# Embedding matmuls moved into the expert groups of a hybrid decoder step, eight expert pieces loaded beside the ring instead of six

## What is computed

```python
h = h + mix
h = h + hier_moe(rmsnorm(h, norm_ffn[i]), ...)
h = h + (p[i] @ ple_w_in[i]) * jax.nn.sigmoid(rmsnorm(h, ple_g[i]) @ ple_w_gate[i])
# in hier_moe: a group of 8 experts by argmax, the top 2 in it, then
a = jnp.einsum('btd,edf->btef', h, w_gate)
u = jnp.einsum('btd,edf->btef', h, w_up)
return jnp.einsum('btef,efd->btd', jax.nn.silu(a) * u * gates[..., None], w_down)
```

## Time and profile before

| | |
|---|---|
| median of 3 runs | 950.71 us (944.7 to 959.28) |
| profiled execution | 951.04 us, span 949.3 us |
| mean granted TensorE clock | 0.921 of 2.4 GHz |
| PE busy | 785.6 us, 83% |
| DVE, ACT, POOL busy | 321.6, 206.6, 56.2 us |
| moved by DMA | 269.32 MB, mean 284 GB/s |

### The profile page before, as it was taken

The page is one execution under the profiler, slowest core; times in us unless marked ns, Lnnn a source line. Parts: engine busy times, 40 slices in busy tenths (PEclk is TensorE's granted clock), DMA queues, the critical chain, the costliest instruction groups (busy, mean ns, idle before and its releaser), DMA issues.

```text
span 949.3 us, 16693 instructions
## 1 busy us (share of the span) xinstructions
PE 785.6 (83%) x6434; PEld 569.2 (60%) x6434; DVE 321.6 (34%) x948; ACT 206.6 (22%) x490; POOL 56.2 (6%) x95
## 2 busy tenths in 40 slices
PE   5899889999777796989997685798998787878894
PEld 4767568765453464667774362587755455545683
DVE  1512333523131331255265272226232231313435
ACT  2100131621111111132135251015211110111222
POOL 3300000000000000000033232000000000000000
PEclk9989998999988988999999796799998898899997
DMA  9941826499999999974319164468699999999501
GB/s 370 368 111 51 266 76 257 164 394 408 415 417 416 415 418 415 419 317 137 129 58 348 33 222 154 164 235 314 271 401 421 414 418 417 416 415 416 220 1 46
DMA packets 59613, 269.32 MB, mean 284 GB/s; under 512 B 7312, under 2 KB 12704, under 8 KB 38416
## 3 DMA queue, kind: packets, MB, share of 16 engines
q1 hardware_dynamic: 53088, 259.31, 69.1%
q10 hardware_dynamic: 3856, 5.40, 1.9%
q0 software_dynamic: 2592, 3.54, 1.2%
HBM read 261.05 MB, written 2.52 MB: 278 GB/s over the span
## 4 chain that ended last, share of the span: by engine, by line
PE 49%; DMA 26%; issue 13%; POOLq 4%; DVE 4%; ACT 2%; ACTq 1%; POOL 1%; SPq 1%; DVEq 0%
DMA ring<-in_moe_w_up 22%; PE bank L623 15%; PE bank L483 13%; PE bank L602 6%; POOLq L1857 3%; PE bank L649 3%; PE bank L507 3%; PE bank L664 2%; DMA arena<-in_stateT 2%; PE bank L892 2%; DMA arena<-arena 1%; PE bank L544 1%; PE bank L558 1%; POOLq L1859 1%; POOLq L1856 1%
## 5 line engine op out<-in xcount | busy, mean ns | idle before, releaser
L623 PE MATMUL bank<-ring,arena 128*32 128x256 f32 x2048 | 148.2, 436 | 62.6 <-DMA ring<-in_moe_w_up 60.2
L623 PEld LDWEIGHTS bank<-ring,arena 128*32 128x32 f32 x2048 | 86.5, 125 | 129.9 <-issue 107.6
L483 PE MATMUL bank<-xn_sq,ring 128*128 128x264 f32 x480 | 109.8, 391 | 10.3 <-DVE xn_sq L996 10.3
L483 PE MATMUL bank<-arena,ring 128*128 128x264 f32 (+1 forms) x456 | 108.7, 399 | 6.5 <-ACT arena L1597 4.0
L483 PEld LDWEIGHTS bank<-xn_sq,ring 128*128 128x128 f32 x480 | 92.2, 193 | 27.1 <-issue 11.1
L1229 DVE TENSOR_TENSOR arena<-arena,bank 128x128 f32<-128x128 f32 x34 | 9.8, 288 | 287.7 <-ACT arena L1638 287.7
L483 PEld LDWEIGHTS bank<-arena,ring 128*128 128x128 f32 x456 | 89.8, 198 | 23.4 <-issue 7.0
L602 PEld LDWEIGHTS bank<-arena 128*128 128x128 f32 x864 | 97.9, 192 | 9.4 <-issue 9.4
L602 PE MATMUL bank<-arena 128*128 128x128 f32 (+1 forms) x864 | 101.1, 277 | 2.0 <-DVE arena L1199 2.0
L649 PE MATMUL bank<-ring,arena 128*32 128x512 f32 x512 | 65.4, 598 | 16.6 <-ACT arena L1645 16.4
L664 PE MATMUL bank<-arena 128*128 128x264 f32 (+1 forms) x288 | 70.7, 399 | 4.7 <-ACT arena L1654 4.7
(11 more groups left out here) (243 smaller groups left out, 799.1 us busy)
## 6 DMA issues: line engine op xcount, KB each, us to landing
ring<-in_moe_w_gate SPq DMA_DIRECT2D x60, 1024.0 KB, 13.9
ring<-in_moe_w_up SPq DMA_DIRECT2D x60, 1024.0 KB, 10.8
ring<-in_moe_w_down SPq DMA_DIRECT2D x60, 1024.0 KB, 12.9
ring<-in_stream SPq DMA_DIRECT2D x35, 1024.0 KB, 14.4
ring<-in_cache_ckv SPq DMA_DIRECT2D x32, 256.0 KB, 7.4
arena<-in_moe_w_down SPq DMA_DIRECT2D x4, 1024.0 KB, 13.4
arena<-in_cache_ckv SPq DMA_DIRECT2D x16, 256.0 KB, 4.3
xn_sq<-in_cache_ckv SPq DMA_DIRECT2D x16, 256.0 KB, 6.1
```

Source lines behind the costliest of these rows:

```text
L483: t = mm(ps[:, 0:cols], lhs(k), rhs(k), start=(k == 0), stop=(k == n - 1))
L623: t = mm(bank[2 + r][p0:p0 + U, 0:F].rearrange("p (c f) -> p c f", c=2), x, w[i][:, :, k * F + c * P:k * F + (c + 1) * P], start=(k == 0), ...
```

## The change

The embedding weights leave the ring. They have an array of their own (`a["pin"]`) and are loaded in the expert stage, behind ring piece i = 26 (`PIN_AT`), into arena buffer 5, once expert 5 is used. The embedding matmuls leave the router part and stand in groups 3 to 6, two chunks each, between `down(a)` and `gate_up(b)`. They write banks 6 and 7, and `pinT` now lies over arena buffers 3 and 4. ACT copies the two chunks behind `pair_out(a)`, and `combine(j)` and the final embedding wait for the copies.

The room of `pinT` and 952 columns more in the arena give six arena buffers instead of four. `ASIDE` has eight pieces: expert 3, the down piece of expert 2, gate and up of expert 5, gate and up of expert 4. The ring list has 88 pieces for 90: i = 6 and 7 are gate and up of expert 2, i = 8 and 9 the down pieces of experts 4 and 5, and the blocks of six begin at i = 10. Ahead of the stage nine ring pieces and eight aside are loaded, 17 for 15. The six in the arena are issued after the last taps of layer 0 (after the first output chunk of attention in layer 1) instead of behind the last output chunk. Four small router tables move into the used tap table `wq`.

```diff
--- before.py
+++ after.py
@@ -44,7 +44,7 @@
 NSLOT = 9
-ARENA = 21888
+ARENA = 22840
@@ -82,12 +82,12 @@
-MOE_PIECES = both(0) + [(e, c) for e in (2, NSTAT) for c in range(3)]
+MOE_PIECES = both(0) + [(2, 0), (2, 1), (4, 2), (5, 2)]
 for _e in range(NSTAT + 1, E, 2):
 RING_AT = {piece: i for i, piece in enumerate(MOE_PIECES)}
-ASIDE = [(3, 0), (3, 1), (3, 2), (4, 2), (4, 0), (4, 1)]
+ASIDE = [(3, 0), (3, 1), (3, 2), (2, 2), (5, 0), (5, 1), (4, 0), (4, 1)]
...
@@ -225,9 +225,11 @@
         gatesT, q = place(q, 2, T)
-        pinT, q = place(q, KD, T)
-        aside, q = place(q, 4, SLOT)
-        assert q <= ARENA
+        aside_at = q
+        aside, q = place(q, 6, SLOT)
+        assert q <= ARENA, q
+        pinT, _ = place(aside_at + 3 * SLOT, KD, T)
+        win = aside[:, 5, :].rearrange("p (k f) -> p k f", k=2)
         aside_x = xn_sq[:].rearrange("p a b c -> p (a b c)")[:, 0:2 * SLOT].rearrange("p (c f) -> p c f", c=2)
...
@@ -415,20 +420,20 @@
-            if e in (3, 4):
-                return aside[:, 0:2, :] if e == 3 else aside_x
+            if e in (3, 4, 5):
+                return {3: aside[:, 0:2, :], 4: aside_x, 5: aside[:, 4:6, :]}[e]
             i = (G_MOE[l] + RING_AT[e, 0]) % NSLOT
-            if e in (3, 4):
-                return aside[:, e - 1, :]
+            if e in (2, 3):
+                return aside[:, 5 - e, :]
             return slot(G_MOE[l] + RING_AT[e, 2])
-            if e in (3, 4):
+            if (e, c) in ASIDE:
                 eng.wait_ge(s_aside[e, c], 16 * (l + 1))
@@ -558,16 +563,6 @@
-                win = slot(G_PIN[l]).rearrange("p (k f) -> p k f", k=2)
-
-                def pin(ms):
-                    for m in ms:
-                        chunk(("pin", l, m), 2, lambda k: win[:, k, m * P:(m + 1) * P], lambda k: pT[:, l, k, :])
-
-                pe.wait_ge(s_p, 16)
-                landed(pe, G_PIN[l])
-                pin(range(5))
-
                 ps = open_bank(pe, ("cnt", l))
@@ -582,8 +577,6 @@
                 t.then_inc(is_full(("rank", l)), 1)
-                pin(range(5, KD))
-
                 for b in range(8):
@@ -650,9 +643,23 @@
+                def pin(j):
+
+                    pe.wait_ge(s_win, 16 * (l + 1))
+                    pe.wait_ge(s_p, 16)
+                    pe.wait_ge(s_add, KD * (gb + j - 1) + 6)
+                    for x in range(2):
+                        m = 2 * (j - 3) + x
+                        for k in range(2):
+                            t = mm(bank[6 + x][:, 0:T], win[:, k, m * P:(m + 1) * P], pT[:, l, k, :], start=(k == 0),
+                                   stop=(k == 1))
+                        t.then_inc(s_pin, 1)
+
                 def combine(j):
                     n = cols_of(j)
+                    if 3 <= j < 7:
+                        pe.wait_ge(s_pinned, KD * l + 2 * (j - 2))
                     pe.wait_ge(s_out, 2 * (pb + min(2 * j + 2, NPR)))
@@ -680,6 +687,8 @@
                     down(a)
+                    if 3 <= j < 7:
+                        pin(j)
                     gate_up(b)
@@ -1356,6 +1365,7 @@
                 name = "n3" if l == 0 else "n6"
+                dve.wait_ge(s_pinned, KD * (l + 1))
                 for m in range(KD + 1):
@@ -1613,12 +1623,8 @@
                          .then_inc(is_free(key), 1)
-                for m in range(5):
-                    pin_in(l, m)
                 act.wait_ge(s_pre, l + 1)
                 s.activation(ex[:], ex[:], ACT.Exp).then_inc(s_ex, 1)
-                for m in range(5, KD):
-                    pin_in(l, m)
                 pb, gb = NPR * l, NGR * l
@@ -1675,6 +1681,14 @@
                     pair_out(a)
+                    if 3 <= j < 7:
+                        if j == 3:
+                            act.wait_ge(s_dn, pb + 2)
+                            act.wait_ge(s_gu, pb + 3)
+                        for x in range(2):
+                            m = 2 * (j - 3) + x
+                            act.wait_ge(s_pin, KD * l + m + 1)
+                            s.copy(pinT[:, m, :], bank[6 + x][:, 0:T]).then_inc(s_pinned, 1)
                     silu(b)
@@ -1944,22 +1951,23 @@
                 e, c = ASIDE[i]
-                d = aside_x[:, c, :] if i >= 4 else aside[:, i, :]
+                d = aside_x[:, c, :] if i >= 6 else aside[:, i, :]
                 if c == 2:
-                for i in range(NSLOT - 1):
+                for i in range(5):
                     load_expert(l, i, MOE_PIECES[i][0])
-                arrive(sp, (("pw2" if l == 0 else "wo"), KD - 1))
-                for i in range(4):
+                arrive(sp, ("taps", KD - 1) if l == 0 else ("wo", 0))
+                for i in range(6):
                     load_aside(l, i)
+                for i in range(5, NSLOT):
+                    load_expert(l, i, MOE_PIECES[i][0])
                 arrive(sp, ("row", l, 2, 1))
-                for i in range(4, 6):
+                for i in range(6, 8):
                     load_aside(l, i)
-                load_expert(l, NSLOT - 1, MOE_PIECES[NSLOT - 1][0])
                 sp.wait_ge(s_perm, l + 1)
@@ -1967,6 +1975,10 @@
                     load_expert(l, i, number[e])
+                    if i == PIN_AT:
+                        sp.wait_ge(s_dn, NPR * l + 2)
+                        sp.wait_ge(s_gu, NPR * l + 3)
+                        sp.dma_start(aside[:, 5, :], a["pin"][l]).then_inc(s_win, 16)
...
@@ -1985,7 +1997,7 @@
                     load_cache(SB * B + i, numbers[i])
-            for g in range(G_PIN1 - 1, G_MOE1):
+            for g in range(G_MOE1 - 1, G_MOE1):
                 fill(g)
```

34 lines of the change are left out of this document (16 added, 18 removed).

## The result

The changed kernel takes 960.72 us, the median of 4 runs (957.9 to 963.78). The kernel before took 950.17 us beside it (4 runs, 944.7 to 959.28). The ratio is 1.0139, with a 95% interval of 1.0088 to 1.0189: slower, by less than 2%. The ratio compares only executions in the faster of the two states that the chip shows, so it is not the quotient of the two medians. The profiled execution took 961.9 us, its span 959.8 us, at a mean granted clock of 0.924. The forecast of 954 had the sign, but a third of the size: +3.4 us were forecast, against +10.5 us by these medians and +10.9 us by the two profiled executions.

The account below looks back on a forecast made before the run. Expert stages were taken as bound by DMA loads, restarting after the router part. Per layer -1.3 (start) and +3.0 (DMA) give +1.7, +3.4 for two layers: 954 us from 950.7; own range 950 to 959, 8 in 10 within 945 to 961.

Parts of the forecast that it names:

- the cold gather: First gather behind the router part: starts at half clock after TensorE idles, costing 1.7 us a layer (0 to 2.0).
- the DMA side of the stream: Expert stage, from the restart of the loads to pair 15: 3.0 us longer per layer (3.0 to 4.0).
- Counts 3.0 us earlier: Router part: without the embedding matmuls ahead of them, the count matmuls start 3.0 us sooner in each layer.
- Router gain: Router part: expert loads restart 1.3 us earlier per layer, 3.0 us from earlier counts less 1.7 for the slow gather.
- The hole: Expert loads after the restart: the ninth waits for pair 2's down matmuls and lands 7.95 us after the eighth, 5.4 lost.
- Early loads: Six arena pieces loaded earlier, at 112 us and about 614 us, where DMA has room: zero cost.
- Embedding matmuls in the stage: Groups 3 to 6: four matmuls of 1.85 us per group fit in the DMA wait ahead of gate_up(b), zero cost.
- Embedding weights at 2.5 us: Expert stage, behind piece 26: loading the embedding weights adds one transfer, 2.5 us per layer.
- Outside the stages: All time outside the router part and the expert stream: no term in the sum, forecast difference 0.
- clock holds: Rival for the router part: full clock through the short matmuls, -3.0 + 3.0 per layer, total 951, chance 0.17.
- no hole: Rival for the expert loads: the stream never runs dry, -3.8 us per layer, total 943.4, chance 0.13.
- Groups held up: Rival for groups 3 to 6: embedding matmuls and their chain of waits delay the groups, total 970, chance 0.05.

Follow-up runs that it names:

- the fourth experiment: The changed kernel with its six early arena loads issued behind the last output chunk again, as in the kernel before: 960.34 us, ratio 1.0106.

## Why the prediction was off

The mechanisms were right: the counts came sooner, the gather ran cold, the stream had a hole. What failed is the sum. Two of its terms were too small: the cold gather (1.7 us against 2.7) and the DMA side of the stream (3.0 us a layer against 3.6). A third, the time outside the two stages, was put at nothing without a reason. The first two make 2.8 us and are shown by traces and experiments. The third is 1.2 us in the traces, within their scatter; another 3.8 us (11.2 less 7.4) are seen in the timed executions alone, have no place in any trace, and their cause stays open.

- **Counts 3.0 us earlier: right.** From DVE's step on the router's logits to the counts it took 5.1 us instead of 8.0 (8.3 in layer 1). In the two experiments with a warm gather and nothing in its way (unread matmuls; chunks spread) the router part is 2.6 to 3.1 us shorter than in the first profile of before.
- **The cold gather: mechanism right, size wrong.** I took 1.7 us from a gate-up behind a 4.75 us wait, and 2.0 as the upper end. It was 2.7 (8.33 and 8.34 against 5.61). The row I priced it by was one in which the clock came back sooner. Here the low clock held until 182, 5.9 us into the gather, so about half of its 5.6 us of work was done at half speed, and the upper end "half of four slow microseconds" was too small. The end of the ranks was slow too (2.00 us against 1.64). Router gain: 0.5 us a layer in place of 1.3. The Trainium skill's page "TensorE: Matmul & The Clock Gate", section "HAM oscillation — how this bites in real kernels", says that a wait which lets the array fall back makes the next burst start cold. The trace agrees in that the gather starts at a PEclk of 0.50 in both layers, but here the clock had fallen ahead of the wait, during the ranks, and the size of 2.7 us had to come from a run.
- **The hole: right in place and mechanism, low by 0.6 us a layer.** Ninth load 26.70 us behind the first (26.85 forecast), 7.6 us between the landings (7.95), pair 6 17.5 us behind pair 5 (17.6), pair 5 at 53.4 and 53.2 us (242.8 - 189.65 = 53.15 forecast). At pair 15 the DMA side was 3.1 us longer in layer 0 (3.0 forecast) and 3.9 us in layer 1 (202.9 against 199.0). Per layer over all profiles it is 3.6 (3.2 in layer 0, 4.0 in layer 1). The bounds of 3.0 to 4.0 held it, though by its own terms the upper one comes to 4.4: 5.45 us and 1.5 lost, 5.0 saved by two pieces, 2.5 added by the embedding weights.
- **Early loads at nothing: right**, by the stretches of the fourth experiment. **Embedding matmuls in the stage at nothing: right.** The wait ahead of pair 7 is still for DMA (1.69 us left). The forecast that such waits shrink by 1.9 us was off (3.5). **Embedding weights at 2.5 us: right**, 2.4 in the experiment that has only these.
- **Outside the stages: not in the sum at all.** The forecast compared one profiled execution with another to be, and took for granted that the clock elsewhere stays. How much of the difference lies there is not shown: 1.2 us in the mean of the traces, and perhaps the 3.8 us that no trace has.

Of the rivals, "clock holds" and "no hole" are excluded by the windows. "Groups held up" is too, since in groups 3 to 6 every `gate_up(b)` in all four profiles of the changed kernel waits for DMA and nothing else.

Put together: the terms that I had were short by 0.8 (router) and 0.6 (stream) per layer, 2.8 us in all, and the outside of the profiles gives 1.2 more: 3.4 + 2.8 + 1.2 is the 7.4 us of the spans. The other 4 us or so are seen only in the timed executions. The time of 960.72 lies inside the range of 945 to 961, at its very edge, and the forecast's own range of 950 to 959 missed it.

## What to carry to other kernels

A prefetched piece is worth something only if its slot comes free early: in a ring with a strict order of issue, one early slot that holds a late piece stops every load behind it. Sort the prefetched pieces by the time at which they are used up, and put into separate buffers the ones that are used late. Before you take "free" matmuls out of a chain of small steps, ask what the clock does without them; spread over the waits they kept the gather at full speed here, which gave 0.6%. And where a change moves the clock, compare many executions, since one profile of each kernel can be off by as much as the effect.

## What was not expected of the hardware

- The clock fell during TensorE's 32-column matmuls, ahead of the wait of 3.5 us and not in it: PEclk was 1.00 at 170 to 171 and 0.50 at 172 to 173, when TensorE was still at the ranks (170.58 + 2.00). It stayed at 0.50 until 182, 5.9 us into the gather. In the mixer it had come back after about 3 us. All four profiles of the changed kernel show the fall during the ranks, in both layers.
- In layer 1 no long wait stood ahead of the fall. TensorE had idled 0.81 us ahead of the counts and was busy with the ranks when PEclk left 1.00:

```profile
661.20 0.94 PE L571 MATMUL bank<-rt_M,cst 128*128 128x32 f32 x6 [0.81 <-DVE rt_M L1143]
662.00:663.00 1.00, 1.00 (x11) 0.96 (x10) 0.72 (x5) 0.98 (x2) 0.00 (x0) 1.00 0.70 295
663.00:664.00 1.00, 1.00 (x6) 0.85 (x5) 0.86 (x6) 0.88 (x2) 0.00 (x0) 0.56 1.00 426
```

- The same instruction stream shows the slow stretches at other places from one execution to the next. Counted from the span's start, the mixer's output chunks began between 123.4 and 127.0 us in the six profiles of before. The 91 timed executions of before scatter by 4.6 us (standard deviation), those of the changed kernel by 2.3.
- DMA-bound stretches do not always repeat either. Seven of the eight streams of the changed kernel took 206.2 to 206.6 us, the eighth 207.8. In the kernel before the six of layer 1 agree (202.2 to 202.6 us), but those of layer 0 spread from 202.1 to 204.6. By a single pair of profiles the change could have cost anything from 1.5 to 5.7 us in layer 0.
